# Expert stage of a fused diffusion layer: weight buffers of their own, four slab loads and three splits placed in the selection stage, expert 0's one-hot built tile by tile

## The chip, the cores and the metric

One core of one Trainium2 chip runs the whole program in one launch. The metric is the device time of that launch in microseconds; the kernel before has 3 runs with a median of 3424.07 (3421.85 to 3424.37). Engines are named as in the profile: PE is the matrix engine (PEld its weight loads), DVE the vector engine, ACT the scalar engine, POOL the GpSimd engine, and SP the engine that only issues DMAs here.

## The reference, cut to what matters

The layer runs a pooling and attention mixer over 2048 noisy and 128 context tokens, and then an expert-choice mixture of experts. Only the second part is touched:

```
def ec_moe(h, w_router, w_gate, w_up, w_down):
    xf = h.reshape(N, D)                                  # D = 1024
    aff = softmax(xf @ w_router)                          # 16 experts
    cap = CAPACITY_FACTOR * N // N_EXPERTS                # 256 noisy, 16 context tokens
    gates, idx = lax.top_k(aff.T, cap)
    xe = xf[idx]
    hid = silu(einsum(xe, w_gate)) * einsum(xe, w_up)
    ye = einsum(hid, w_down) * gates[..., None]
    out = zeros((N, D)).at[idx.reshape(-1)].add(ye)
```

## The kernel before, in words

Four stages follow one another, each a block that all engines enter and leave together: the head groups (to about 1815 us of the traced execution), the output projection with the router (to 2076), the selection (`stage_select`, L1992) and the experts (`stage_experts`, L2209).

**Selection.** For every expert the threshold of its 256 best tokens is found bit by bit, three bits a round, in ten rounds. One round on DVE: a comparison of 2048 affinities with a bound, with their count (L2102), the same for the 128 context tokens, a comparison of the two counts with the capacities (`ind`, L2105), a small matmul on PE (L2196), and then `digit` (L2109), `bound` (L2112) and `cand` (L2114), which the next round's comparison waits for (`settled`). `ind`, `bound` and `cand` each read two operands from SBUF and touch 2 elements a partition. After the rounds come masks, ranks by PE, and `g.place`, the slot of every token at every expert. POOL makes the constants, clears the semaphores of the stage before, and is then idle; ACT makes three copies (L2161) and is idle; SP has nothing to do.

**Experts.** Each of the 16 experts has 12 weight slabs of 1024 x 256 values (4 pairs of gate and up, 4 of down), 1 MB each. SP loads slab s into one of RAW = 4 places of `raw` (L2306). For float32 precision each slab is split in two halves: ACT casts it to the high part (L2475), then DVE subtracts that from the slab for the low part (L2567), into one of RING = 3 places of `w`. PE needs both (`w_lo`). SP loads a slab once the slab four before it has been split.

Before expert 0 can start, its tokens have to be found and fetched. DVE makes `hot`, for 16 tiles at once a comparison of the 256 slot numbers with `g.place` (`one_hot(0)`, L2531), then `hot_p`, `vcur` and `hot_all` (L2622, the context tokens of all experts). PE multiplies `hot` and `vcur` to a list of tokens (`make_list`, L2352), DVE turns it into indices (`read_list`, L2547), and POOL gathers the 256 rows by two indirect DMAs (L2321). PE meanwhile picks the context tokens of all experts (`pick`, L2365), split by ACT (L2479) and DVE (`picked`, L2573), transposes the gathered rows (`turn`, L2378), and ACT (L2491) and DVE (L2578) split them into `xT`. Only then come the main matmuls (L2405): 48 a slab.

The order of this beginning is written out by hand for each engine. On DVE: `one_hot(0)`, `hot_all`, `read_list(0)`, four `picked`, two slab splits, four `turned`. On ACT: four `picked`, two slab casts, `place_prompt`, four `turned`. On SP: the loads of `h2p` (0.5 MB) and of `gate2` (twice 0.5 MB), then slabs 0 to 3. The buffers `raw`, `w`, `h2p` and `gate2` are allocated inside the expert stage.

Of the kernel before, what the change touches and what calls it, by code (L numbers as in the profile page):

```python
# [20 lines left out]
F32 = mybir.dt.float32  # L21
F32R = mybir.dt.float32r
BF16 = mybir.dt.bfloat16
U32 = mybir.dt.uint32
ALU = mybir.AluOpType
# [37 lines left out]
def clear_spent(pool, sems):  # L63

    for s in sems:
        pool.sem_clear(s)
# [1922 lines left out]
            run_tiles(pool, body)  # L1989


def stage_select(nc, g, held):  # L1992


    ROUNDS, STEPS = 10, 8
# [1 line left out]
    with ExitStack() as ctx:  # L1997
# [41 lines left out]
        spent, g.spent = g.spent, sems  # L2039
        block = ctx.enter_context(nc.Block())  # L2040

        def over_tiles(x, n):
            return x.rearrange("p (o e) -> p o e", o=1).broadcast_to([P, n, NE])

        @block.gpsimd
        def _(pool):
            nc.gpsimd.iota(lane[:], [[1, P]], base=P, channel_multiplier=-1).then_inc(made_lanes, 1)
            nc.gpsimd.iota(offset[:, 0:1], [[0, 1]], base=0, channel_multiplier=1).then_inc(made_lanes, 1)
            for n, value in enumerate((1.0, float(RATIO))):
                nc.gpsimd.memset(ones[:, n, :], value).then_inc(set_up, 1)  # L2050
            pool.wait_ge(set_up, 2)
            for n in range(2):
                nc.gpsimd.affine_select(out=tri[:, n, :], in_=ones[:, n, :], compare_op=ALU.is_gt, fill=0.0, base=0,
                                        pattern=[[1, P]], channel_multiplier=-1).then_inc(tri_made, 1)
            nc.gpsimd.iota(g.slots[:], [[1, CAP]], base=1, channel_multiplier=0,
                           allow_small_or_imprecise_dtypes=True).then_inc(iotas, 1)
            nc.gpsimd.iota(g.vals[:, :, :, 0], [[0, NT], [0, NE]], base=0, channel_multiplier=1,
                           allow_small_or_imprecise_dtypes=True).then_inc(iotas, 1)
            nc.gpsimd.iota(g.vals[:, :, :, 1], [[1, NT], [0, NE]], base=0, channel_multiplier=0,
                           allow_small_or_imprecise_dtypes=True).then_inc(iotas, 1)  # L2060
            nc.gpsimd.memset(g.tile_off[:], 0.0).then_inc(iotas, 1)
            pool.wait_ge(iotas, 4)
            nc.gpsimd.memset(g.tile_off[:, 0:1], float(T)).then_inc(iotas, 1)
            clear_spent(pool, spent)

        @block.vector
        def _(dve):
# [88 lines left out]
        @block.scalar  # L2156
        def _(act):
            for n in (0, 2, 4):
                act.wait_ge(turned, n + 1)
                src = ps_w[:, n, :] if n < 4 else ps_rp[:, 0:P]  # L2160
                nc.scalar.copy(affT[:, 512 * n:min(512 * n + 512, NT * P)], src).then_inc(turned_s, 1)  # L2161

        @block.tensor
        def _(pe):
# [44 lines left out]
def stage_experts(nc, g, io, outs):  # L2209


    SLABS = 12
    RAW, RING = 4, 3
    TILES = ((0, P), (CAPP, P), (CAPP + P, P))
    sems = []
    with ExitStack() as ctx:  # L2216
        def sb(name, shape, dt=F32):
            return ctx.enter_context(nc.sbuf_tensor(name, shape, dt))
# [2 lines left out]
            sems.append(ctx.enter_context(nc.semaphore(name)))  # L2221
            return sems[-1]

        raw = sb("e_raw", [P, RAW, 2048])
        w = sb("e_w", [P, RING, 2, 2048], F32R)
        hot = sb("hot", [P, NS, CAP], BF16)
        hot_p = sb("hot_p", [P, CAPP], BF16)
        vcur = sb("vcur", [P, NT, 5], BF16)
        found = sb("found", [P, 3, 5])
        gsum = sb("gsum", [P, 3])  # L2230
# [3 lines left out]
        i_cur = sb("i_cur", [P, 3], U32)  # L2234
        xg = sb("xg", [P, 2, D])

        h2p = sb("h2_prompt", [P, D])
        hot_all = sb("hot_all", [P, NE, CAPP])
        xTp = sb("xT_prompt", [P, NE, 2, KD, CAPP], F32R)
        xT = sb("xT", [P, 2, KD, SLOTS], F32R)  # L2240
# [2 lines left out]
        hid = sb("hid", [P, 2, KD, SLOTS], F32R)  # L2243
        yT = sb("e_yT", [P, 2, 2, SLOTS])
        y = sb("e_y", [P, 3, D])
        gate2 = sb("gate2", [P, 2, D])
        ps_gu = ctx.enter_context(nc.psum_tensor("ps_gu", [P, 4, 512], F32))
        ps_d = ctx.enter_context(nc.psum_tensor("ps_d", [P, 3, 512], F32))
        ps_x = ctx.enter_context(nc.psum_tensor("ps_x", [P, 512], F32))

        raw_in = [sem(f"raw_in{q}") for q in range(RAW)]
        w_hi, w_lo, slab_done = sem("e_whi"), sem("e_wlo"), sem("slab_done")
        gate2_in = sem("gate2_in")
        moved, hot_done, listed, found_done, idx_done, gs1, gs2 = (
            sem(n) for n in ("e_moved", "hot_done", "listed", "found_done", "idx_done", "gs1", "gs2"))
        gathered, xT_ready, xT_hi, xT_lo = sem("gathered"), sem("exT_ready"), sem("exT_hi"), sem("exT_lo")
        h2p_in, hot_all_done, xT_placed = sem("h2p_in"), sem("hot_all_done"), sem("exT_placed")
        xTp_ready, xTp_hi, xTp_lo = sem("xTp_ready"), sem("xTp_hi"), sem("xTp_lo")
        silu_done, h32_done, hid_hi, hid_lo = (sem(n) for n in ("silu_done", "eh32_done", "hid_hi", "hid_lo"))
        yT_ready, yT_copied, yT_turned = sem("yT_ready"), sem("yT_copied"), sem("yT_turned")  # L2260
# [28 lines left out]

        @block.sync  # L2290
        def _(sp):
            sp.dma_start(h2p[:], g.h2[NS * P:NT * P, :]).then_inc(h2p_in, 16)
            sp.dma_start(gate2[:, 0, :], g.mod[0, 5 * D:6 * D].partition_broadcast(P)).then_inc(gate2_in, 16)
            sp.dma_start(gate2[:, 1, :], g.mod[1, 5 * D:6 * D].partition_broadcast(P)).then_inc(gate2_in, 16)

            def body(e, before, more):
                for s in range(SLABS):
                    n = SLABS * e + s
                    wait_positive(sp, w_lo, n - RAW + 1)
                    if not isinstance(e, int):  # L2300
                        sp.sem_inc(passed, 1)
                    name, q = ("w_down", s - 8) if s >= 8 else ("w_gate" if s % 2 == 0 else "w_up", s // 2)
                    src = io[name][0].rearrange("e (k p) n -> e p k n", p=P)
                    src = src[bass.ds(e, 1), :, :, 256 * q:256 * q + 256]
                    dst = raw[:, s % RAW, :].rearrange("p (k n) -> p k n", n=256)
                    sp.dma_start(dst, src.rearrange("o p k n -> (o p) k n")).then_inc(raw_in[s % RAW], 16)  # L2306

            run_experts(sp, body)

# [36 lines left out]
        def _(pe):  # L2346
# [45 lines left out]
            def body(e, before, more):  # L2392
# [51 lines left out]
                if not more:  # L2444
                    turn_back(e, 3)

            make_list(0)
            for p in range(PAIRS):
                pick(p)
            for p in range(PAIRS):  # L2450
                turn(0, p)
            pe.wait_ge(xTp_lo, PAIRS)
# [12 lines left out]
        def _(act):  # L2465
            def split(e, s, more):

                if s >= SLABS:
                    if not more:
                        return  # L2470
                    e, s = e + 1, s - SLABS
                wait_positive(act, raw_in[s % RAW], 16 * (3 * e + s // RAW + 1))
                if not (isinstance(e, int) and e == 0 and s < RING):
                    wait_read(act, e, s - RING)
                nc.scalar.copy(w[:, s % RING, 0, :], raw[:, s % RAW, :]).then_inc(w_hi, 1)  # L2475

            def picked(p):
# [37 lines left out]

            for p in range(PAIRS):
                picked(p)
            for s in range(2):
                split(0, s, True)
            place_prompt(0)  # L2520
            for p in range(PAIRS):
                turned(0, p)
# [3 lines left out]
        def _(dve):  # L2526
            def one_hot(e):

                wait_positive(dve, listed, e)
                at = g.place[:, :, bass.ds(e, 1)]  # L2530
                nc.vector.tensor_tensor(hot[:], g.slots[:].rearrange("p (o c) -> p o c", o=1).broadcast_to([P, NS, CAP]),  # L2531
                                        at[:, 0:NS].broadcast_to([P, NS, CAP]), ALU.is_equal).then_inc(hot_done, 1)
                nc.vector.tensor_tensor(hot_p[:], g.slots[:, 0:CAPP],
                                        at[:, NS].broadcast_to([P, CAPP]), ALU.is_equal).then_inc(hot_done, 1)
                nc.vector.tensor_copy(vcur[:], g.vals[:, :, bass.ds(e, 1), :].rearrange("p t o c -> p t (o c)")
                                      ).then_inc(hot_done, 1)

            def read_list(e):

# [19 lines left out]
                nc.vector.tensor_copy(g_cur[:], g_next[:]).then_inc(moved, 1)  # L2559

            def split(e, s, more):
                if s >= SLABS:
                    if not more:
                        return
                    e, s = e + 1, s - SLABS
                wait_positive(dve, w_hi, SLABS * e + s + 1)
                nc.vector.tensor_tensor(w[:, s % RING, 1, :], raw[:, s % RAW, :], w[:, s % RING, 0, :].bitcast(F32),  # L2567
                                        ALU.subtract).then_inc(w_lo, 1)
# [25 lines left out]
            def body(e, before, more):  # L2594
# [22 lines left out]
                    result(e, 1)  # L2617

            nc.vector.memset(found[:], float(NS)).then_inc(found_set, 1)
            dve.wait_ge(found_set, 1)  # L2620
            one_hot(0)
            nc.vector.tensor_tensor(hot_all[:], g.slots[:, 0:CAPP].rearrange("p (o c) -> p o c", o=1).broadcast_to(  # L2622
                [P, NE, CAPP]), g.place[:, NS, :].rearrange("p (e o) -> p e o", o=1).broadcast_to([P, NE, CAPP]),
                ALU.is_equal).then_inc(hot_all_done, 1)
            read_list(0)
            for p in range(PAIRS):
                picked(p)
            for s in range(2):
                split(0, s, True)
            for p in range(PAIRS):  # L2630
                turned(0, p)
            dve.wait_ge(gate2_in, 32)
# [3 lines left out]
def build(nc, io, outs, stop=None):  # L2636
# [7 lines left out]
    with ExitStack() as ctx:  # L2644
# [14 lines left out]
        g.tile_off = sb("tile_off", [P, 3])  # L2659
        stage_output(nc, g, io, outs, after_output)  # L2660
        after_heads.close()
        stage_select(nc, g, after_select)
        after_output.close()
        stage_experts(nc, g, io, outs)
        after_select.close()
# [53 lines left out]
```

## Time and profile before

| | us |
|---|---|
| median of 3 runs | 3424.07 |
| span of the profiled execution | 3423.3 |
| PE busy in it | 3208.2 |
| DVE busy | 2301.4 |
| ACT busy | 1633.2 |
| POOL busy | 633.3 |
| selection stage (start of its first work to the experts' first) | 2076.3 to 2128.7 |
| experts' beginning, to the first main matmul | 2128.7 to 2151.1 |

The span runs from the first to the last instruction of the profiled execution; 0.8 us lie between it and the median of the runs. Times of single instructions below are microseconds from the span's start. "Idle before" with an arrow names what the engine waited for. The granted TensorE clock is given as a share of its full 2.4 GHz, so 0.50 is 1.2 GHz.

### The profile page before, as it was taken

How to read it: one execution, taken by the hardware profiler on the slowest of the kernel's cores; microseconds unless marked ns; L12 is line 12 of the kernel's file. 1: busy time of each engine (PE TensorE's matmuls, PEld its weight loads, DVE VectorE, ACT ScalarE, POOL GpSimd, SP SyncE). 2: the span in 40 equal slices, each digit the busy share in tenths (PEclk: the TensorE clock that was granted, in tenths of full speed). 3: DMA queues.
4: the chain of work that ended last, by engine and by line, in shares of the span. 5: the costliest groups of instructions: out<-in, count | busy, mean ns of one | idle time of the engine just before them, and what ended most of it. 6: DMA issues, size and time to landing. Idle time of an engine off the chain costs nothing. (4 is left out here: it accounts for less than half of the span.)

```text
span 3423.3 us, 69668 instructions
## 1 busy us (share of the span) xinstructions
PE 3208.2 (94%) x23738; PEld 2997.6 (88%) x23738; DVE 2301.4 (67%) x3793; ACT 1633.2 (48%) x3631; POOL 633.3 (18%) x854
## 2 busy tenths in 40 slices
PE   6879999999999999998987993999999999999997
PEld 4879988998998998997775883999999999999997
DVE  4778878877887887887884446555565555555553
ACT  3436656666665665665552110444444444444442
POOL 2432233232223223321000000000110000000001
PEclk8989999999999999999998995999999999999998
DMA  8554444444345435442325551666666666666663
GB/s 281 204 197 141 125 123 151 122 127 152 121 119 157 122 122 165 120 124 93 101 71 220 191 190 57 212 187 185 185 185 195 191 194 194 185 185 185 185 187 86
DMA packets 357398, 542.47 MB, mean 158 GB/s; under 512 B 26266, under 2 KB 280730, under 8 KB 342042
## 3 DMA queue, kind: packets, MB, share of 16 engines
q1 hardware_dynamic: 347548, 506.30, 45.8%
q0 software_dynamic: 9728, 34.61, 4.4%
q8 instruction: 68, 1.11, 0.1%
q14 instruction: 54, 0.44, 0.0%
HBM read 439.10 MB, written 101.74 MB: 158 GB/s over the span
## 5 line engine op out<-in xcount | busy, mean ns | idle before, releaser
L2405 PE MATMUL ps_gu<-xT,e_w 128*128 128x272 f32 x6144 | 789.2, 290 | 2.5 <-DVE xT L2578 2.5
L2405 PEld LDWEIGHTS ps_gu<-xT,e_w 128*128 128x128 f32 x6144 | 779.8, 189 | 3.2 <-issue 2.9
L2567 DVE TENSOR_TENSOR e_w<-e_raw,e_w 128x2048 fp32r<-128x2048 f32 x192 | 440.1, 2292 | 418.1 <-ACT e_w L2475 403.0
L1040 ACT ACTIVATE e<-ps_s,negm 128x1024 f32<-128x1024 f32 (+2 forms) x416 | 473.8, 1145 | 221.4 <-DVE negm L1374 221.4
L1366 DVE TENSOR_REDUCE mx<-ps_s 128x1 f32<-128x1024 f32 (+3 forms) x428 | 521.7, 1232 | 69.0 <-PE ps_s L703 67.5
L703 PE MATMUL ps_s<-kT,qT 128*128 128x512 f32 (+1 forms) x1920 | 469.2, 384 | 12.2 <-ACT e L1040 11.6
L743 PE MATMUL ps_m<-v,aT 128*128 128x128 f32 x3456 | 473.4, 280 | 6.2 <-ACT aT L1028 3.6
L743 PEld LDWEIGHTS ps_m<-v,aT 128*128 128x128 f32 x3456 | 422.6, 192 | 35.2 <-issue 14.6
L703 PEld LDWEIGHTS ps_s<-kT,qT 128*128 128x128 f32 x1920 | 346.9, 190 | 83.9 <-ACT e L1040 17.4
L2424 PE MATMUL ps_gu<-hid,e_w 128*128 128x272 f32 x3072 | 412.1, 291 | 0.0
L773 PE MATMUL ps_m<-w,hT 128*128 128x384 f32 x2040 | 392.8, 340 | 3.9 <-DVE o L1423 3.9
L2424 PEld LDWEIGHTS ps_gu<-hid,e_w 128*128 128x128 f32 x3072 | 392.5, 188 | 0.0
L2475 ACT CAST e_w<-e_raw 128x2048 fp32r<-128x2048 f32 x192 | 365.4, 1903 | 2.7 <-DMA e_raw<-w_up 0.8
L773 PEld LDWEIGHTS ps_m<-w,hT 128*128 128x128 f32 x2040 | 349.9, 188 | 5.4 <-issue 5.4
L1359 DVE SCALAR_TENSOR_TENSOR e<-e,coef 128x512 f32<-128x512 f32 (+1 forms) x480 | 309.7, 693 | 3.4
L1028 ACT COPY aT<-ps_t 128x512 f32<-128x512 f32 (+2 forms) x390 | 203.4, 531 | 210.5 <-PE ps_t L724 210.1
L724 PE MATMUL ps_t<-ident,e 128*128 128x128 f32 x1728 | 270.9, 277 | 13.2 <-DVE e L1359 9.4
L724 PEld LDWEIGHTS ps_t<-ident,e 128*128 128x128 f32 x1728 | 199.5, 141 | 42.4 <-DVE e L1359 24.0
L1885 PE MATMUL ps_y<-wo,cat_o 128*128 128x512 f32 x816 | 199.3, 401 | 19.5 <-DMA cat_o<-cat_d 17.2
L1885 PEld LDWEIGHTS ps_y<-wo,cat_o 128*128 128x128 f32 x816 | 154.0, 192 | 52.4 <-DMA cat_o<-cat_d 18.0
L1253 POOL TENSOR_TENSOR r<-ms,nhalf 128x4 f32<-128x4 f32 x102 | 110.4, 1082 | 473.9 <-ACT ms L1052 473.7
L2504 ACT CAST hid<-e_h 128x544 fp32r<-128x544 f32 x64 | 41.5, 648 | 316.6 <-DVE e_h L2610 316.6
(286 smaller groups left out, 3395.5 us busy)
## 6 DMA issues: line engine op xcount, KB each, us to landing
hT<-hT_d SPq DMA_DIRECT2D x85, 1024.0 KB, 5.6
e_raw<-w_gate SPq DMA_DIRECT2D x64, 1024.0 KB, 5.3
e_raw<-w_up SPq DMA_DIRECT2D x64, 1024.0 KB, 5.2
e_raw<-w_down SPq DMA_DIRECT2D x64, 1024.0 KB, 7.4
qT_d<-qT_out SPq DMA_DIRECT2D x96, 256.0 KB, 5.6
qT<-qT_d SPq DMA_DIRECT2D x96, 256.0 KB, 2.8
tab<-tabs_d SPq DMA_DIRECT2D x85, 256.0 KB, 2.7
hT_d<-hT SPq DMA_DIRECT2D x17, 1024.0 KB, 3.9
```

Of the source, the lines that this page charges most:

```text
L703: mm = nc.tensor.matmul(ps_s[:, at + x - lo:at + y - lo], lhs, keys, start=(half == 0), stop=(half == 1))
L724: mm = nc.tensor.transpose(ps_t[:, n % 2, m * P:m * P + P], src[:, b * P:b * P + P], g.ident[:])
L743: mm = nc.tensor.matmul(ps_m[:, 0:P], aT[:, n % 2, m * P:m * P + P], vals, start=(b == 0), stop=(b == last))
L773: mm = nc.tensor.matmul(projected(s), hT[:, s.par, a, k, :], w[:, s.h % 2, b, k, :], start=(k == 0 and a + b == 0), stop=(k == KD - 1 and ...
L1040: nc.scalar.activation(out, src, ACT.Exp, bias=negm[:, s.par, c:c + 1], scale=HD ** -0.5, accum_out=acc).then_inc(exp_done.sem, 1)
L1359: nc.vector.scalar_tensor_tensor(a, b, coef[:], a, ALU.mult, ALU.add).then_inc(mixed.sem, 1)
L1366: nc.vector.tensor_reduce(mx[:, c, n:n + 1], ps_s[:, at:at + hi - lo], AX, ALU.max).then_inc(mx_part.sem, 1)
L1885: mm = nc.tensor.matmul(ps_y[:, par, half, :], cat[:, par, k, a, :], w[:, b, k, 512 * half:512 * half + 512], start=(k == 0 and a + b == 0 ...
L2405: mm = nc.tensor.matmul(ps_gu[:, 2 * (s % 2) + f, 0:SLOTS], w_view(s, a)[:, k, f * P:f * P + P], xT[:, b, k, :], start=(k == 0 and a + b = ...
L2424: mm = nc.tensor.matmul(ps_gu[:, 2 * (d % 2) + f, 0:SLOTS], w_view(s, a)[:, k, f * P:f * P + P], hid[:, b, k, :], start=(k == 0 and a + b ...
L2475: nc.scalar.copy(w[:, s % RING, 0, :], raw[:, s % RAW, :]).then_inc(w_hi, 1)
L2567: nc.vector.tensor_tensor(w[:, s % RING, 1, :], raw[:, s % RAW, :], w[:, s % RING, 0, :].bitcast(F32), ALU.subtract).then_inc(w_lo, 1)
```

## The change

`open_weights` allocates `e_raw`, `e_w`, `h2_prompt`, `gate2` and their semaphores before the selection stage, in memory that the selection doesn't use. In the selection, SP issues the loads of slabs 0 to 3, of `h2p` and of `gate2`; ACT casts slabs 0 to 2 behind its three copies; POOL, behind its clearing of semaphores, makes the low parts of slabs 0 to 2 (DVE's work before). In the expert stage these are left out, so SP begins with slab 4. DVE makes `hot_all` first, copies expert 0's places to `place_0`, and builds `hot` by 16 instructions of one tile each with a per-partition scalar. PE does `pick(0)` and `pick(1)` before `make_list(0)`; DVE does `picked(0)` before `read_list(0)`.

```diff
+RAW, RING, EARLY = 4, 3, 3
+def open_weights(nc, g, ctx):
+    g.raw = ctx.enter_context(nc.sbuf_tensor("e_raw", [P, RAW, 2048], F32))
+    g.ew = ctx.enter_context(nc.sbuf_tensor("e_w", [P, RING, 2, 2048], F32R))
+    g.h2p = ctx.enter_context(nc.sbuf_tensor("h2_prompt", [P, D], F32))
+    g.gate2 = ctx.enter_context(nc.sbuf_tensor("gate2", [P, 2, D], F32))
...
 def stage_select(...):
+        @block.sync
+        def _(sp):
+            for s in range(RAW):
+                sp.dma_start(g.raw[:, s, :].rearrange("p (k n) -> p k n", n=256), slab_source(io, 0, s)
+                             ).then_inc(g.raw_in[s], 16)
+            sp.dma_start(g.h2p[:], g.h2[NS * P:NT * P, :]).then_inc(g.h2p_in, 16)
+            sp.dma_start(g.gate2[:, 0, :], g.mod[0, 5 * D:6 * D].partition_broadcast(P)).then_inc(g.gate2_in, 16)
+            sp.dma_start(g.gate2[:, 1, :], g.mod[1, 5 * D:6 * D].partition_broadcast(P)).then_inc(g.gate2_in, 16)
...
             clear_spent(pool, spent)
+            for s in range(EARLY):
+                pool.wait_ge(g.w_hi, s + 1)
+                nc.gpsimd.tensor_tensor(g.ew[:, s, 1, :], g.raw[:, s, :], g.ew[:, s, 0, :].bitcast(F32),
+                                        ALU.subtract).then_inc(g.w_lo, 1)
...
+            for s in range(EARLY):
+                act.wait_ge(g.raw_in[s], 16)
+                nc.scalar.copy(g.ew[:, s, 0, :], g.raw[:, s, :]).then_inc(g.w_hi, 1)
...
 def stage_experts(...):
-            sp.dma_start(h2p[:], ...)
-            sp.dma_start(gate2[:, 0, :], ...)
-            sp.dma_start(gate2[:, 1, :], ...)
-                for s in range(SLABS):
+                for s in range(0 if before else RAW, SLABS):
...
+            pick(0)
+            pick(1)
             make_list(0)
-            for p in range(PAIRS):
-                pick(p)
+            pick(2)
+            pick(3)
...
             def split(e, s, more):                      # on ACT and on DVE
+                if isinstance(e, int) and e == 0 and s < EARLY:
+                    return
...
-            for s in range(2):                          # on ACT and on DVE
-                split(0, s, True)
...
+            def first_hot():
+                for t in range(NS):
+                    ins = nc.vector.tensor_scalar(hot[:, t, :], g.slots[:], place_0[:, t:t + 1], None, ALU.is_equal)
+                ins.then_inc(hot_done, 1)
+                nc.vector.tensor_tensor(hot_p[:], g.slots[:, 0:CAPP], g.place[:, NS, 0:1].broadcast_to([P, CAPP]),
+                                        ALU.is_equal).then_inc(hot_done, 1)
+                nc.vector.tensor_copy(vcur[:], g.vals[:, :, 0, :]).then_inc(hot_done, 1)
...
-            dve.wait_ge(found_set, 1)
-            one_hot(0)
             nc.vector.tensor_tensor(hot_all[:], ...).then_inc(hot_all_done, 1)
+            nc.vector.tensor_copy(place_0[:], g.place[:, 0:NS, 0]).then_inc(found_set, 1)
+            dve.wait_ge(found_set, 2)
+            first_hot()
+            picked(0)
             read_list(0)
-            for p in range(PAIRS):
+            for p in range(1, PAIRS):
                 picked(p)
```

## Rows read from the trace of the kernel before

**Rows 1.** The page's first part: busy time of each engine.
```profile
PE 3208.2 (94%) x23738; PEld 2997.6 (88%) x23738; DVE 2301.4 (67%) x3793; ACT 1633.2 (48%) x3631; POOL 633.3 (18%) x854
```

**Rows 2.** The chain of waits from the experts' start, in order of time.
```profile
2130.49 13.66 DMA e_raw<-w_up
...
2144.17 1.91 ACT e_w L2475
...
2146.10 2.29 DVE e_w L2567
...
2151.05 33.12 PE ps_gu L2405 x240
```

**Rows 3.** Busy time by stretch: start:end, length, PE, PEld, DVE, ACT, POOL, clock, DMA, GB/s.
```profile
2090.00:2100.00 10.00, 0.56 (x3) 0.31 (x3) 9.00 (x25) 0.00 (x0) 0.00 (x0) 0.50 0.00 0
...
2151.00:2156.90 5.90, 5.86 (x26) 5.89 (x27) 2.29 (x1) 1.22 (x1) 0.00 (x0) 0.50 1.09 350
2156.90:2160.00 3.10, 3.10 (x26) 3.10 (x26) 0.00 (x0) 0.01 (x1) 0.00 (x0) 0.99 0.48 154
```

**Rows 4.** Timeline of DVE, first of the ten selection rounds: start, length, what.
```profile
2081.72 2.35 DVE L2102 TENSOR_SCALAR_CACHE_REDUCE passing<-affT,bound 128x2048 bf16<-128x2048 f32 x1
...
2084.50 0.16 DVE L2105 TENSOR_TENSOR ind<-count_s,caps 128x2 bf16<-128x2 f32 x1
...
2085.20 0.22 DVE L2112 SCALAR_TENSOR_TENSOR bound<-digit,offset,cand 128x2 uint32<-128x2 uint32 x1
2085.34 0.15 DVE L2114 TENSOR_TENSOR cand<-digit,cand 128x2 uint32<-128x2 uint32 x1
```

**Rows 5.** The page's sixth part: loads of a slab, median us to landing.
```profile
e_raw<-w_gate SPq DMA_DIRECT2D x64, 1024.0 KB, 5.3
```

**Rows 6.** Timeline of ACT: its idle time before its first work for the experts.
```profile
2136.69 0.59 ACT L2479 CAST xT_prompt<-ps_d 128x512 fp32r<-128x512 f32 x1 [55.36 <-issue]
```

**Rows 7.** Groups of instructions on POOL, shapes apart: busy, mean ns of one.
```profile
L1270 POOL TENSOR_TENSOR sinp<-qkn,tab 128x128 f32<-128x128 f32 x204 | 90.4, 465 | 0.0
...
L1264 POOL TENSOR_TENSOR cosp<-qkn,tab 128x256 f32<-128x256 f32 x102 | 75.0, 735 | 466.6 <-DVE qkn L1387 466.6
```

**Rows 8.** Line 1535 alone: instructions with the least, median and longest ns.
```profile
L1535 DVE TENSOR_TENSOR e<-e,edge x16: 157/164/669, 105.9 to 244.5; 64x8 f32<-64x8 f32 x16
```

**Rows 9.** Timelines of DVE and of POOL, 226.0 to 228.2.
```profile
226.45 0.91 DVE L1537 SCALAR_TENSOR_TENSOR e<-e,inv_w 64x512 f32<-64x512 f32 x1
227.39 0.59 DVE L1535 TENSOR_TENSOR e<-e,edge 64x8 f32<-64x8 f32 x1
...
225.47 1.34 POOL L1270 TENSOR_TENSOR sinp<-qkn,tab 128x128 f32<-128x128 f32 x2
226.94 1.01 POOL L1278 TENSOR_TENSOR rot<-cosp,sinp 128x256 f32<-128x256 f32 x1
```

**Rows 10.** Timeline of SP: the first load of the expert stage.
```profile
2128.67 0.34 SPq L2292 DMA_DIRECT2D h_prompt<-h_d  x1
```

**Rows 11.** Timeline of DVE: a copy in the selection, then the experts' one-hots.
```profile
2076.39 0.69 DVE L2083 COPY wide<-aff 128x1024 f32<-128x1024 f32 x1
...
2128.85 4.42 DVE L2531 TENSOR_TENSOR hot<-slots,place 128x4096 bf16<-128x4096 bf16 x1
...
2133.39 0.41 DVE L2622 TENSOR_TENSOR hot_all<-slots,place 128x256 f32<-128x256 bf16 x1
```

**Rows 12.** Timeline of POOL: the second of the two gathers for expert 0.
```profile
2136.93 0.96 POOL L2321 DMA_INDIRECT xg<-h_d,i_next  x1 [0.30 <-issue]
```

**Rows 13.** The gathered tile `xg`, all 16 experts: issue to landing.
```profile
DMA to landing us min/median/max: 4.9/5.3/7.9
```

**Rows 14.** Timelines of PE and of ACT: transposes of expert 0's rows, last copy.
```profile
2144.82 3.68 PE L2378 MATMUL ps_gu<-ident,xg 128*128 128x128 f32 x16 [3.92 <-DMA xg<-h_d,i_next]
...
2148.54 0.59 ACT L2491 CAST xT<-ps_gu 128x512 fp32r<-128x512 f32 x1 [0.27 <-PE ps_gu L2378]
```

**Rows 15.** Timeline of DVE: the splits of expert 0's rows.
```profile
2148.31 2.48 DVE L2578 TENSOR_TENSOR xT<-ps_gu,xT 128x512 fp32r<-128x512 f32 x4
```

More of the change, by code:

```diff
@@ L1989, in _, with slab_source, stage_select @@
             run_tiles(pool, body)
-def stage_select(nc, g, held):
+RAW, RING, EARLY = 4, 3, 3
[4 more added lines that the diff above has]
+    g.gate2 = ctx.enter_context(nc.sbuf_tensor("gate2", [P, 2, D], F32))
+    g.raw_in = [ctx.enter_context(nc.semaphore(f"raw_in{q}")) for q in range(RAW)]
+    g.w_hi, g.w_lo, g.h2p_in, g.gate2_in = (
+        ctx.enter_context(nc.semaphore(n)) for n in ("e_whi", "e_wlo", "h2p_in", "gate2_in"))
+def slab_source(io, e, s):
+    name, q = ("w_down", s - 8) if s >= 8 else ("w_gate" if s % 2 == 0 else "w_up", s // 2)
+    src = io[name][0].rearrange("e (k p) n -> e p k n", p=P)
+    return src[bass.ds(e, 1), :, :, 256 * q:256 * q + 256].rearrange("o p k n -> (o p) k n")
+def stage_select(nc, g, io, held):
     ROUNDS, STEPS = 10, 8
@@ L2212, in stage_experts @@
     SLABS = 12
-    RAW, RING = 4, 3
     TILES = ((0, P), (CAPP, P), (CAPP + P, P))
@@ L2222, in sem @@
             return sems[-1]
-        raw = sb("e_raw", [P, RAW, 2048])
-        w = sb("e_w", [P, RING, 2, 2048], F32R)
+        raw, w, h2p, gate2 = g.raw, g.ew, g.h2p, g.gate2
         hot = sb("hot", [P, NS, CAP], BF16)
         hot_p = sb("hot_p", [P, CAPP], BF16)
+        place_0 = sb("place_0", [P, NS])
         vcur = sb("vcur", [P, NT, 5], BF16)
@@ L2235, in stage_experts @@
         xg = sb("xg", [P, 2, D])
-        h2p = sb("h2_prompt", [P, D])
         hot_all = sb("hot_all", [P, NE, CAPP])
@@ L2245, in stage_experts @@
         y = sb("e_y", [P, 3, D])
-        gate2 = sb("gate2", [P, 2, D])
         ps_gu = ctx.enter_context(nc.psum_tensor("ps_gu", [P, 4, 512], F32))
@@ L2249, in stage_experts @@
         ps_x = ctx.enter_context(nc.psum_tensor("ps_x", [P, 512], F32))
-        raw_in = [sem(f"raw_in{q}") for q in range(RAW)]
-        w_hi, w_lo, slab_done = sem("e_whi"), sem("e_wlo"), sem("slab_done")
-        gate2_in = sem("gate2_in")
+        raw_in, w_hi, w_lo, h2p_in, gate2_in = g.raw_in, g.w_hi, g.w_lo, g.h2p_in, g.gate2_in
+        sems.extend(raw_in + [w_hi, w_lo, h2p_in, gate2_in])
+        slab_done = sem("slab_done")
         moved, hot_done, listed, found_done, idx_done, gs1, gs2 = (
@@ L2256, in stage_experts @@
         gathered, xT_ready, xT_hi, xT_lo = sem("gathered"), sem("exT_ready"), sem("exT_hi"), sem("exT_lo")
-        h2p_in, hot_all_done, xT_placed = sem("h2p_in"), sem("hot_all_done"), sem("exT_placed")
+        hot_all_done, xT_placed = sem("hot_all_done"), sem("exT_placed")
         xTp_ready, xTp_hi, xTp_lo = sem("xTp_ready"), sem("xTp_hi"), sem("xTp_lo")
@@ L2291, in _ @@
         def _(sp):
-            sp.dma_start(h2p[:], g.h2[NS * P:NT * P, :]).then_inc(h2p_in, 16)
-            sp.dma_start(gate2[:, 0, :], g.mod[0, 5 * D:6 * D].partition_broadcast(P)).then_inc(gate2_in, 16)
-            sp.dma_start(gate2[:, 1, :], g.mod[1, 5 * D:6 * D].partition_broadcast(P)).then_inc(gate2_in, 16)
             def body(e, before, more):
-                for s in range(SLABS):
+                for s in range(0 if before else RAW, SLABS):
                     n = SLABS * e + s
@@ L2301, in body @@
                         sp.sem_inc(passed, 1)
[L2302 to L2306, printed above, removed]
+                    sp.dma_start(raw[:, s % RAW, :].rearrange("p (k n) -> p k n", n=256), slab_source(io, e, s)
+                                 ).then_inc(raw_in[s % RAW], 16)
             run_experts(sp, body)
@@ L2472, in split @@
                 wait_positive(act, raw_in[s % RAW], 16 * (3 * e + s // RAW + 1))
-                if not (isinstance(e, int) and e == 0 and s < RING):
-                    wait_read(act, e, s - RING)
+                wait_read(act, e, s - RING)
                 nc.scalar.copy(w[:, s % RING, 0, :], raw[:, s % RAW, :]).then_inc(w_hi, 1)
@@ L2561, in split @@
             def split(e, s, more):
+                if isinstance(e, int) and e == 0 and s < EARLY:
+                    return
                 if s >= SLABS:
@@ L2624, in _ @@
                 ALU.is_equal).then_inc(hot_all_done, 1)
+            nc.vector.tensor_copy(place_0[:], g.place[:, 0:NS, 0]).then_inc(found_set, 1)
+            dve.wait_ge(found_set, 2)
+            first_hot()
+            picked(0)
             read_list(0)
-            for p in range(PAIRS):
+            for p in range(1, PAIRS):
                 picked(p)
-            for s in range(2):
-                split(0, s, True)
             for p in range(PAIRS):
@@ L2661, in build @@
         after_heads.close()
-        stage_select(nc, g, after_select)
+        open_weights(nc, g, ctx)
+        stage_select(nc, g, io, after_select)
         after_output.close()
```

## The prediction

> **What bounds the kernel now.** The page comes first: PE is busy for 94% of the span, so most of the program is not at stake [rows 1]. The change touches two stretches in which PE has little to do, and each has its own limit. In the selection the view by stretch shows DVE busy 9.00 of 10 us and PE 0.56: ten rounds in which one small DVE instruction waits for the one before [rows 3]. Whatever delays one of them delays the program. In the experts' beginning the chain of waits names the weights: the second slab landed 13.66 us after its issue, ACT cast it (1.91), DVE split it (2.29), DVE's four splits of the tokens followed, and the main matmuls began at 2151.05 [rows 2]. From there PE runs without a gap (240 matmuls in 33.12 us, the first ones slow by their clock), so only what comes before 2151.05 can be gained.
>
> **What the early weights save.** Loads, casts and splits of slabs 0 and 1 leave the chain. Next in line is the gather. Its rows were there at 2144.82, when PE began 3.68 us of transposes, and ACT's last copy ended at 2149.13 [rows 14]. One of DVE's four splits costs 2.48 / 4 = 0.62 [rows 15]; with 0.25 for the start of PE this gives 2150.0, that is 5.2 after the landing. Today's 2151.05 is thus 1.05 later than the gather alone would give, and this much is sure. The rest hangs on when the gather lands.
>
> Its issue hangs on the list, and that on `hot`, 4.42 us for 4096 elements, one element a cycle [rows 11]. In its place stand `hot_all` first (0.41 busy, some 0.34 until the next can start), a copy of 16 elements (0.2) and 16 instructions of 256 elements. No row has this form. By the rate of `hot`, 4.42 / 16 = 0.28 and some 0.06 of start make 0.34 each, 5.4 in all, and the list 1.6 later; by the copy of 1024 elements in 0.69, two elements a cycle, it is 0.14 and 0.06, 3.2 in all, and the list 0.6 earlier. The new form has one tensor input, as that copy has, so I take 3.2 (down to 2.2 if it ran at twice that rate, which nothing in the rows excludes). The Trainium skill (VectorE: DVE Perf Modes, Mode 4×_2P) says that a tensor_scalar whose tensors are all 16-bit and in SBUF goes at four elements a cycle; by it the list is some 1.6 earlier. The trace has no such instruction.
>
> The second gather goes out at 2136.93 and landed 7.9 later, the longest of 32; the median is 5.3 [rows 12, 13]. What made it long was 5.5 MB queued in front and around it from 2128.67 on [rows 10]. Now `h2p`, `gate2` and four slabs are already there, but SP does not wait: the splits of slabs 0 to 2 are done, so slabs 4 to 6, 3 MB, go out at 2128.67. At the 350 GB/s of [rows 3] they keep the DMA engines busy to about 2139, and the gather, issued at 2136.3, still meets them. So its wait lies between 4.9 and 7.9; I take 6.0, and the landing at 2142.3 (2141.2 to 2144.2). With the 5.2 from above the main matmuls start 2147.5 after an unchanged selection: **3.5 us earlier**, between 1.5 and 5.5.
>
> At no cost: two `pick`s before the list (four matmuls of 256 columns, some 1.8 us by the 3.68 for twice as many columns in [rows 14]; PE waits for `hot` at that time, also if it took 2.2 only); `picked(0)` before `read_list` (0.69, under the list's matmuls); ACT's three casts, 5.7 us inside an idle time of 55.4 [rows 6]; SP's seven issues in a stage where it does nothing. Slab 3 and all later ones are split under PE's work as before, and with three more slabs loaded ahead nothing there gets later.
>
> The clock: from 2151.0 to 2156.9 the granted clock was 0.50, then 0.99, and 26 matmuls took 5.90 and 3.10 us [rows 3]; the low stretch therefore costs 2.9. PE's pattern before it (picks, a gap, transposes, a gap) stays much the same, so I leave it at no change; at best 2.9 come back, at worst another 0.5 goes.
>
> **What the early splits cost.** DVE's subtraction is now POOL's, during the rounds. POOL needs 465 ns for 128 columns and 735 for 256 [rows 7], hence 2.11 ns a column, and for 2048 columns 465 + 1920 x 2.11 = 4.5 us; three take 13.5. POOL is idle then, and they end far ahead of the stage. What counts is what DVE does meanwhile. Line 1535 shows it: an instruction with two inputs in SBUF on 8 columns, 164 ns as a rule and once 669 [rows 8]. [Rows 9] show one such place. The one at 227.39 took 0.59 and ended at 227.98, just behind POOL's 256 columns of 226.94, which ended at 227.95. Those took 1.01 in place of 0.735, as they had themselves met DVE's instruction of 226.45 to 227.36, and that had begun beside POOL's pair, which ended at 226.81. I read this as turns: whoever comes second waits for the whole instruction, however small its own.
>
> In a selection round `ind`, `bound` and `cand` have two SBUF inputs [rows 4]. The first slab lands 5.3 after its issue at 2076.3 [rows 5], ACT casts it in 1.9, so POOL's first subtraction starts near 2083.5; the other casts (one each 3 us, the time of 1 MB at 350 GB/s) are ready before POOL wants them. Then:
> - POOL 2083.5 to 2088.0: `ind`, due at 2084.50, waits 3.5.
> - POOL's second to 2092.6: `bound`, due 0.7 after `ind`, waits 3.9.
> - POOL's third to 2097.1: `cand`, queued behind `bound`, waits 4.5.
>
> Together **11.9 us**, all on the chain, since PE and the next comparison wait for them. The bounds: nothing, if tiny DVE instructions slip in between POOL's accesses; 14, if the long comparison (one SBUF input and a count) is held as well. If `bound` and `cand` pass together between two subtractions, or POOL starts some 2 us later, the comparison of 2.35 runs beside POOL and about 3 are saved: 8 to 9. On that upper bound the Trainium skill (SBUF — State Buffer, Who interferes with whom) says that a tensor_scalar which also writes its accumulator doesn't compete with GpSimd; by it the 14 is ruled out. No row shows such an instruction beside POOL's work, so the bound stays.
>
> **Sum.** 3423.3 + 11.9 - 3.5 = 3431.7 for the profiled execution; the median of the runs shown lies 0.8 above that execution's span, so **3432.5**. A measurement of this kernel can tell some 0.2%, 6.8 us, from no change, so 3430.9 is where "slower" begins.
>
> **The rivals.**
> 1. POOL and DVE don't hold each other here (not slower). The places in [rows 9] are few and short; if a long subtraction of POOL lets instructions of 2 elements through, the cost of the selection vanishes and the prologue's gain stays: 3424.1 - 3.5 = 3420.6. It decides from the point at which the rounds lose less than 3.5 us. Against it: the 8-column instruction that waited. 12%.
> 2. They hold each other less than in the sum: the comparison covers part of each subtraction, 8 us, and the gather lands near the median: 3424.1 + 8 - 4.5 = 3427.6. 25%.
> 3. The change doesn't shorten the gather: slabs 4 to 6 stand in front of it just as slabs 0 to 3 did, 7.9 again, landing at 2144.2, and only some 1.6 are gained: 3424.1 + 11.9 - 1.6 = 3434.4. For it: the queue was full at that moment too. 18%.
> 4. The clock rises before the main matmuls and the selection isn't held: 3420.6 - 2.9 = 3417.7, just over 0.2% faster only with the best gather as well. 5%.
>
> The forecast, 3432.5, has 40%.
>
> **How the numbers follow.** The forecast's own range is 3429 to 3436. The held cases reach from 3425 to 3437.5; to hold the time 8 times in 10 I go down to 3420.5, rival 1's time, as its sign is the other. Slower by over 0.2% are rival 3, most of the forecast and a little of rival 2: 0.58. Faster by over 0.2% is the best part of rival 4: 0.05. The rest, 0.37, is within.
>
> **What would show it.** In the profile after: POOL's three subtractions of 128x2048 at some 4.5 us each between 2083 and 2098; `ind`, `bound` or `cand` of the first round or two with 3 to 4.5 us in place of 0.2; the experts' first load near 2140.6 for 2128.7 [rows 10]; between this and the first main matmul 18.9 us for 22.4, with PE's transposes waiting for the gather, not for weights; `hot` as 16 instructions at 0.2 us from start to start. Wrong would be: rounds that keep their pace beside POOL's work (then rival 1), or a main stage that now waits for slab 3 or later.

## The result, and the profile after

The changed kernel takes 3428.09 us (median of 20 runs, 3424.22 to 3432.61) where the kernel before took 3423.81 (20 runs, 3420.26 to 3426.88): ratio 1.0014, 95% interval 1.0008 to 1.0020. It is slower, by 4.3 us, which lies within the 0.2% that were called "no change". The forecast was 3432.5. The profiled execution has a span of 3428.6, against 3423.3.

First the page's part on busy time, for [rows 1], then DVE's timeline of the first selection rounds, for [rows 4]:

```profile
PE 3205.6 (93%) x23738; PEld 2994.9 (87%) x23738; DVE 2301.1 (67%) x3806; ACT 1633.7 (48%) x3631; POOL 643.8 (19%) x857
```
```profile
2085.50 3.82 DVE L2139 TENSOR_TENSOR ind<-count_s,caps 128x2 bf16<-128x2 f32 x1
...
2089.86 3.92 DVE L2146 SCALAR_TENSOR_TENSOR bound<-digit,offset,cand 128x2 uint32<-128x2 uint32 x1
2093.70 0.15 DVE L2148 TENSOR_TENSOR cand<-digit,cand 128x2 uint32<-128x2 uint32 x1
...
2096.67 1.58 DVE L2139 TENSOR_TENSOR ind<-count_s,caps 128x2 bf16<-128x2 f32 x1
```

The busy totals hide it. POOL has 10.5 us more, for its three subtractions; DVE has as much as before, as three of its own subtractions went away (2.29 us each, [rows 2]) and the time that it was held counts as busy. Three small instructions show all: 0.16, 0.22 and 0.16 us before, 3.82, 3.92 and 1.58 now, together 8.8 more. POOL's timeline has its subtractions beside them, and the second gather, for [rows 12]:

```profile
2084.80 13.43 POOL L2097 TENSOR_TENSOR e_w<-e_raw,e_w 128x2048 fp32r<-128x2048 f32 x3 [3.71 <-ACT e_w L2198]
...
2146.03 0.96 POOL L2348 DMA_INDIRECT xg<-h_d,i_next  x1 [0.30 <-issue]
```

The subtractions took 4.5 us each, ending at 2089.3, 2093.8 and 2098.2, and so did `ind`, `bound` and the next `ind`. The experts' beginning, by the chain of waits (for [rows 2]) and by DVE's and SP's timelines (for [rows 11, 10]):

```profile
2146.03 6.29 DMA xg<-h_d,i_next
...
2152.37 3.69 PE ps_gu L2405 x16
2156.08 0.59 ACT xT L2521
2156.70 0.70 DVE xT L2617
...
2157.64 32.30 PE ps_gu L2432 x240
```
```profile
2138.50 0.42 DVE L2659 TENSOR_TENSOR hot_all<-slots,place 128x256 f32<-128x256 bf16 x1 [0.58 <-PEq L2018]
...
2139.04 3.22 DVE L2569 TENSOR_SCALAR hot<-slots,place 128x256 bf16<-128x256 bf16 x16
```
```profile
2138.43 0.38 SPq L2332 DMA_DIRECT2D e_raw<-w_gate  x1
2138.86 0.57 SPq L2332 DMA_DIRECT2D e_raw<-w_up  x1
2139.49 1.38 SPq L2332 DMA_DIRECT2D e_raw<-w_gate  x1
```

No slab is on the chain any more; the gather is. From the start of each stage to the next (DVE's first instruction of a stage, PE's first main matmul), in us:

| | selection | beginning | first main matmul to expert 1's list |
|---|---|---|---|
| before | 52.4 | 22.3 | 33.0 |
| after | 61.15 | 19.15 | 32.1 |
| difference | +8.75 | -3.15 | -0.8 |

These make 4.8 of the span's 5.3; the selection also started 1.0 later, and 0.5 came back behind expert 0, in parts that the change doesn't touch. The second and third of these times move from execution to execution: two more profiles of the kernel before (numbers 9 and 10) have beginnings of 21.5 and 22.1, so the beginning gained 2.3 to 3.2, not exactly 3.15. The selection doesn't move (52.4 each time).

### The profile page after: what moved, and what is told of

Its sections match the earlier page's. It is cut to its first block and busy times, and to the rows that moved or that the text cites. A ratio compares the mean times of both kernels' runs of the same rounds, so it can differ in the third digit from the quotient of the medians.

```text
span 3428.6 us, 69684 instructions
## 1 busy us (share of the span) xinstructions
PE 3205.6 (93%) x23738; PEld 2994.9 (87%) x23738; DVE 2301.1 (67%) x3806; ACT 1633.7 (48%) x3631; POOL 643.8 (19%) x857
## 5 line engine op out<-in xcount | busy, mean ns | idle before, releaser
L2606 DVE TENSOR_TENSOR e_w<-e_raw,e_w 128x2048 fp32r<-128x2048 f32 x189 | 433.0, 2291 | 417.8 <-ACT e_w L2505 417.8
```

## The experiments

Every kernel here is compared with the runs of the kernel before on its own chip. The three durations are measured as in the table above, each in one profile; "after the stage's start" means after DVE's first instruction of the expert stage. Lines that a diff leaves out are marked by `...`.

**1. The low parts made by DVE again.** POOL's loop is left out, the early loads and casts stay, and DVE's `split` no longer skips slabs 0 to 2.

```diff
-            for s in range(EARLY):                  # POOL, in the selection
-                pool.wait_ge(g.w_hi, s + 1)
-                nc.gpsimd.tensor_tensor(...)
...
-            for p in range(1, PAIRS):               # DVE, in the expert stage
-                picked(p)
+            picked(1)
+            split(0, 0, True)
+            picked(2)
+            picked(3)
+            split(0, 1, True)
```

> The changed kernel without POOL's three subtractions: the slabs are still loaded and cast early, but DVE makes the low parts, of slabs 0 and 1 between its splits of the context tokens (where it is idle for 1.3 and 5.3 us now, waiting for ACT and for the gather) and of slab 2 in the loop. Theory (POOL's subtractions hold DVE's small instructions, and that is the whole loss): all ten rounds back at 3.74 us, selection 52.3 us instead of 61.1, and 8.8 us off the changed kernel's time; from the experts' start to the main matmuls 18 to 19.5 us, as SP now waits for DVE's first split before it loads slab 4, and the gather meets fewer loads. Median some 3418.5 to 3420, faster than both. Rival (the early DMA traffic or ACT's casts slow the rounds): the rounds stay at their loss of 8.8 or a part of it, and the time stays at 3426 or above.

Measured: selection 52.39, no instruction held, so the early traffic and ACT's casts cost nothing, and POOL's subtractions are the whole loss. But the time was 3421.39 (11 runs; before 3422.67; ratio 0.9994, 0.9985 to 1.0003), which can't be told from the kernel before, and the beginning took 20.37, 0.9 above the range that was expected. The timelines of POOL, DVE and SP say why:

```profile
2136.99 2.09 POOL L2344 DMA_INDIRECT xg<-h_d,i_next  x1 [0.30 <-issue]
...
2135.97 2.28 DVE L2600 TENSOR_TENSOR e_w<-e_raw,e_w 128x2048 fp32r<-128x2048 f32 x1
...
2138.28 0.38 SPq L2328 DMA_DIRECT2D e_raw<-w_gate  x1
```

Now DVE holds POOL: the making of the second gather took 2.09 in place of 0.96 beside a DVE subtraction that ended at 2138.25, and PE's transposes began 15.1 after the stage's start, not 13.9. Of this 1.2, the longer making is 1.1. The queue was empty when the gather went out, but didn't stay so: with its first split done SP issued slab 4 at 2138.28, before the making of the gather ended (2139.08). From that end to the transposes it took 5.6 us, for 5.4 in the changed kernel and 4.3 in number 5, where no slab moved meanwhile.

The hold doesn't rest on this one place. At the end of each expert POOL makes indirect DMAs that scatter `y_sample`. In the trace of the kernel before, one such instruction took 3.04 us the first time and 2.29 to 2.31 the 13 later times, always beside a split of DVE that had begun first (timelines of POOL and DVE, two of the places):

```profile
2248.26 3.04 POOL L2332 DMA_INDIRECT y_sample<-e_y,i_cur  x1 [0.31 <-issue]
...
2247.57 2.29 DVE L2567 TENSOR_TENSOR e_w<-e_raw,e_w 128x2048 fp32r<-128x2048 f32 x1 [1.08 <-ACT e_w L2475]
...
2327.11 2.29 POOL L2332 DMA_INDIRECT y_sample<-e_y,i_cur  x1 [0.30 <-issue]
...
2325.67 2.29 DVE L2567 TENSOR_TENSOR e_w<-e_raw,e_w 128x2048 fp32r<-128x2048 f32 x1 [1.08 <-issue]
```

Both end 1.4 us behind the end of DVE's split (2249.87 and 2327.96). Where DVE's subtraction began second, POOL wasn't stretched: the making of the first gather in number 1 took its usual 1.20, though the subtraction began 0.5 into it.

**2. POOL as busy, but only writing.** The low parts of slabs 0 to 2 are zero here.

```diff
-                nc.gpsimd.tensor_tensor(g.ew[:, s, 1, :], g.raw[:, s, :], ..., ALU.subtract)
+                nc.gpsimd.memset(idle[:, s, :], 0.0)
+                nc.gpsimd.memset(g.ew[:, s, 1, :].bitcast(F32), 0.0)
```

> The changed kernel with POOL's subtractions replaced by POOL instructions that only write: per slab one memset of 3072 columns into an unused buffer and one of 2048 into the low part, some 4.5 us a slab as before. The low parts of slabs 0 to 2 are zero, so expert 0's products leave that part out. Theory (DVE instructions with two SBUF inputs compete with POOL's reads alone): the rounds run at 3.74 us beside 13.5 us of POOL work, selection 52.3 us. Rival (any POOL work in SBUF holds them): ind and bound wait 3.5 to 4 us again, selection near 61.

Measured: selection 52.39. POOL was busy beside the rounds (first line, of its timeline), and `ind` and `bound` (of DVE's) took what they always had:

```profile
2079.80 2.66 POOL L2098 MEMSET idle<- 128x3072 f32 x1 [3.63 <-ACT e_w L2199]
...
2080.57 0.16 DVE L2140 TENSOR_TENSOR ind<-count_s,caps 128x2 bf16<-128x2 f32 x1
...
2081.28 0.22 DVE L2147 SCALAR_TENSOR_TENSOR bound<-digit,offset,cand 128x2 uint32<-128x2 uint32 x1
```

So it isn't POOL's work as such. A memset differs from the subtraction in that it reads nothing, and that is the likely reason; a POOL instruction that reads a single input wasn't run. The single time, 3415.0, also holds an early start of the selection (4 us) and a fast expert 0.

**3. Each subtraction in 8 pieces of 256 columns.**

> The changed kernel with each POOL subtraction cut into 8 of 256 columns. Theory (they take turns by whole instructions): ind, bound and cand each wait for one piece at most, 0.7 us and 0.4 on average, in the four or five rounds that POOL's work of 17 us now spans; the selection loses 3 to 7 us, no single wait over 0.9 us. Rival (what counts is POOL's busy time, however it is cut): 8.8 us or more lost.

Measured: selection 55.9, 3.5 us lost in seven waits, the time 3423.8 (one run). DVE's timeline:

```profile
2084.11 0.62 DVE L2141 TENSOR_TENSOR ind<-count_s,caps 128x2 bf16<-128x2 f32 x1
...
2085.26 0.22 DVE L2148 SCALAR_TENSOR_TENSOR bound<-digit,offset,cand 128x2 uint32<-128x2 uint32 x1
2085.40 0.70 DVE L2150 TENSOR_TENSOR cand<-digit,cand 128x2 uint32<-128x2 uint32 x1
...
2090.13 0.74 DVE L2150 TENSOR_TENSOR cand<-digit,cand 128x2 uint32<-128x2 uint32 x1
```

POOL was busy for longer (16.4 us for 13.4) and cost less. No wait exceeds a piece (0.73): they take turns by instructions, and the length of POOL's sets the price.

**4. Halves, started behind `cand` of one of the first six rounds.**

```diff
-            for s in range(EARLY):
...
+            for j in range(2 * EARLY):
+                s, at = j // 2, 1024 * (j % 2)
+                pool.wait_ge(g.w_hi, s + 1)
+                pool.wait_ge(step, 8 + 6 * (j + 1))       # cand of round j
+                ins = nc.gpsimd.tensor_tensor(g.ew[:, s, 1, at:at + 1024], ..., ALU.subtract)
```

> The changed kernel with each POOL subtraction cut in two halves of 1024 columns (2.36 us by 465 + 896 x 2.11 ns), each of them started behind cand of one of the first six rounds, that is beside the comparison of 2048 values with its count (2.35 us and 0.5 more until ind). Theory (only ind, bound and cand are held; the comparison isn't): no wait at all, selection 52.3 us, the experts' beginning as in the changed kernel at 19.2 us: 8.8 us off, median near 3419.3. Rival (the comparison is held as well, as it also reads SBUF): each half adds some 2.4 us, selection near 66 us, median near 3433.

Measured: selection 52.39, beginning 19.14, 3418.81 us (11 runs; before 3422.67; ratio 0.9985, 0.9976 to 0.9994). The timelines of POOL and DVE:

```profile
2085.65 2.35 POOL L2099 TENSOR_TENSOR e_w<-e_raw,e_w 128x1024 fp32r<-128x1024 f32 x1 [5.55 <-DVE cand L2152]
2089.38 2.35 POOL L2099 TENSOR_TENSOR e_w<-e_raw,e_w 128x1024 fp32r<-128x1024 f32 x1 [1.38 <-DVE cand L2152]
...
2085.53 2.35 DVE L2140 TENSOR_SCALAR_CACHE_REDUCE passing<-affT,bound 128x2048 bf16<-128x2048 f32 x1
```

The long comparison ran beside them in the 2.35 us that it takes alone. It isn't held, and the same work on POOL at another moment is free.

**5. Slab 4 held back until the gathered rows are there.**

```diff
+                    if not before and s == RAW:
+                        sp.wait_ge(xT_ready, 1)
```

> The changed kernel with SP holding slab 4 (and so 5 and 6) back until PE has transposed the first pair of expert 0's gathered rows. Theory (the three slabs issued at the stage's start stand in front of the gather; PE's first transpose came 13.9 us after the stage's start, the second gather's issue 7.5): with the DMA engines empty the gather needs 4.0 to 4.9 us from the second issue instead of 6.3, PE's transposes start 11.5 to 12.4 us after the stage's start, and the beginning falls from 19.2 to some 17.2 us. Rival (the gather's own 1 MB and its making on POOL set the time): 13.9 and 19.2 as before. A cost could appear later: a PE wait for slab 4 in expert 0; slab 4 then lands some 18 us after the stage's start and is needed some 40 us after it, so none is expected. The selection keeps its loss of 8.8 us.

Measured: transposes 12.8 after the stage's start, beginning 17.9, selection 61.0, and 3426.4 us in a single run. Of the 2 us expected, 1.2 came: the chain has 5.21 from the second issue to the landing for 6.29. With slabs queued the gather's first bytes come 4.1 us behind the first issue and the rest within 3.1; alone the first come at 1.9, but the rest takes 4.3 (the second half is only issued 1.5 after the first).

**6. Halves and held slab together.**

> Both at once: POOL's subtractions in halves beside the comparisons (selection 52.4 us measured with it) and SP holding slab 4 back. Theory: selection 52.4 and beginning 17.2, so 2 us under the kernel with the timed halves alone (3418.8), near 3416.8, and 6 to 7 us under the kernel before. Rival: holding back gives nothing, 3418.8.

Measured: selection 52.4, beginning 17.9, 3417.72 us (11 runs; before 3424.30; ratio 0.9981, 0.9972 to 0.9990): 6.6 us under the kernel before, the best version here. Over number 4 it gains 1.2 in the beginning; by ratios of the two (0.9981 to 0.9985) that isn't clear of noise.

**7. The one-hot in one instruction again.**

> The changed kernel with expert 0's one-hot as one DVE instruction again, everything else as changed. The 16 instructions took 3.22 us, the one 4.42. Theory: the list and the gather's issue come 1.1 to 1.2 us later (second issue 8.7 instead of 7.5 us after the stage's start), but the gather's first bytes wait for the three slabs anyway (they came 4.1 us after the first issue), so PE's transposes start only 0 to 0.6 later and the beginning takes 19.2 to 19.8. Rival: the delay goes through whole, 20.3.

Measured, DVE's timeline and the chain of waits:

```profile
2139.58 4.43 DVE L2568 TENSOR_TENSOR hot<-slots,place 128x4096 bf16<-128x4096 bf16 x1
```
```profile
2147.60 5.26 DMA xg<-h_d,i_next
```

The second issue came 8.56 after the stage's start in place of 7.53, the transposes at 13.9 and the beginning 19.15, both as in the changed kernel (single run: 3428.9 us). The gather waited a microsecond less in the queue. The tile-by-tile one-hot is faster and gains nothing in this kernel.

**8. The changed kernel once more.**

> The changed kernel once more, unchanged. In its profile cand started 13 ns before POOL's third subtraction and slipped through with bound. If that is a matter of a few ns, it may be held this time (its 0.15 us become some 4.4, and the selection loses 11.9 instead of 8.8); if the order of the two is fixed by how they wait, ind 3.8, bound 3.9, cand 0.15 and the next ind 1.6 come again within 0.3 us.

Measured: selection 60.9, beginning 19.1, 3425.1 us (one run); DVE's timeline:

```profile
2082.23 3.55 DVE L2139 TENSOR_TENSOR ind<-count_s,caps 128x2 bf16<-128x2 f32 x1
2086.32 3.92 DVE L2146 SCALAR_TENSOR_TENSOR bound<-digit,offset,cand 128x2 uint32<-128x2 uint32 x1
2090.16 0.15 DVE L2148 TENSOR_TENSOR cand<-digit,cand 128x2 uint32<-128x2 uint32 x1
2093.12 1.58 DVE L2139 TENSOR_TENSOR ind<-count_s,caps 128x2 bf16<-128x2 f32 x1
```

`cand` began 19 ns ahead of POOL's third subtraction, and 21 and 9 ns in numbers 5 and 7. This order repeats with whole subtractions. It isn't safe, though: in number 3 `cand` twice began 4 and 3 ns ahead of POOL's next piece and was held all the same (0.74 us at 2090.13, the last line shown there).

**9 and 10. The kernel before, twice more, for the clock.**

> The kernel before once more, for the clock in expert 0. From the first main matmul to expert 1's list PE needs 32.96 us in its profile; in the changed kernels it was 32.14 once, 31.95 to 31.74 three times and 30.34 five times. Theory A (where the clock rises is chance, and differs from execution to execution of one kernel): this one differs from 32.96 by over 0.3 us. Theory B (the change moved it): 32.7 to 33.3 again, and the change brought 0.8 to 2.6 us by the clock alone. The selection and the beginning: 52.4 and 22.3 again.

> The same kernel a third time, for the same question: by theory A some value between 30.3 and 33.3 us that needn't agree with the other two, by theory B 32.7 to 33.3.

Measured: 33.1 and 31.85 us, beginnings of 21.5 and 22.1, selections of 52.4, times of 3423.3 and 3423.7 us. Number 9 alone fits theory B; number 10 doesn't. So executions of one kernel differ by 1.2 here, and theory B in its narrow form fails. The changed kernel shows the same, by stretches of 5.4 us from the first main matmul, in the profile above and in number 8:

```profile
2157.60:2163.00 5.40, 5.36 (x28) 5.39 (x29) 0.00 (x0) 0.36 (x1) 0.00 (x0) 0.62 0.01 3
```
```profile
2154.00:2159.40 5.40, 5.34 (x42) 5.37 (x43) 0.00 (x0) 0.38 (x1) 0.00 (x0) 1.00 0.01 3
```

28 matmuls at a granted clock of 0.62, 42 at 1.00, with the same instructions ahead. Yet the shortest value, 30.3, came in five of the nine profiles of changed kernels and in none of three of the kernel before. The time that PE is idle just before the main matmuls doesn't explain it by itself: it is 1.6 to 1.7 us in all nine, and 2.5, 1.6 and 2.9 in the three, where the profile with 1.6 (number 9) has the slowest expert 0. Whether the change makes the short value likelier stays open; three profiles are too few.

## Why the prediction was right or wrong

- **POOL and DVE hold each other by whole instructions**, read from [rows 8, 9]: right, as numbers 1 to 4 show. The first two waits were put at 3.5 and 3.9 and came out at 3.7 and 3.7.
- **"`cand`, queued behind `bound`, waits 4.5"**: this step failed. `cand` starts 9 to 21 ns ahead of POOL's next subtraction, in all four profiles with whole subtractions, and goes through with `bound`. The third subtraction then runs beside the comparison and holds only the end of it, `ind` by 1.4. The cost was 8.75, not 11.9. The text had this case as a variant at 8 to 9, and chose the other by the turns of [rows 9], where DVE's next instruction was not yet waiting.
- **Is the comparison held?** The bound of 14 left that open, and number 4 closes it: it is not. The Trainium skill (SBUF — State Buffer, Who interferes with whom) says so of a tensor_scalar that writes its accumulator, and the trace agrees (2.35 us beside POOL's work).
- **The beginning**: 18.9 forecast, 19.15 measured; gather 6.3 from its second issue for 6.0. Right also in what bounds it: the slabs in front of the gather (number 5), worth 1.1 of the 6.3.
- **The one-hot**: 3.2 forecast, 3.22 measured. At the four elements a cycle that the Trainium skill (VectorE: DVE Perf Modes, Mode 4×_2P) states for such an instruction it would be an estimated 2.2; here, with 16-bit tensors and a float32 scalar per partition, the trace doesn't agree: 0.20 from start to start for 256 elements, as the two elements a cycle of the copy in [rows 11] gave. Not foreseen was that the 0.6 earlier list would be swallowed by the queue (number 7).
- **Two `pick`s at no cost**: right by little, and the reading was wrong. They were put at four matmuls and 1.8 us, so that they'd be free even with a `hot` of 2.2. In the trace they are eight matmuls and take 3.75 us, from 2139.07 to 2142.82, and the list's first matmul began at 2142.61, when `vcur` had ended at 2142.47. With a `hot` of 2.2 they would have held the list up.
- **The clock at no change**: 0.8 less in the profile, within what executions of one kernel differ by. (The slow stretch of [rows 3] costs 5.90 - 3.10 = 2.8, not 2.9; nothing hangs on it.) In the median the loss is 4.3, and 8.75 - 3.15 gives 5.6. The means of three profiles of the kernel before and two of the changed one differ by +8.6 in the selection, -2.8 in the beginning and -1.4 in expert 0, together 4.4. That fits, but how much of it is the clock isn't shown, as the last term moves by over 1 us between executions of one kernel.
- **Sum**: 3432.5 - 3.15 (`cand`) + 0.35 (the beginning) - 0.8 (clock) gives 3428.9, against 3428.09 measured. The sign was right, the 0.2% were not reached. The time lies 0.9 under the forecast's own range (3429 to 3436) and 0.5 from rival 2's 3427.6, which had the selection nearly right (8) and the gather too early (4.5 gained). So the wider range held the time, and not the forecast's sum.

## What to carry to other kernels

Work moved to an idle engine isn't free if the two hold each other when both read SBUF, as VectorE and GpSimd do here: ask what short instructions of the critical engine have two SBUF inputs, and give GpSimd its reads only beside instructions that don't, in pieces no longer than those. When a load is taken off the chain, look at the queue that is next: three slabs prefetched as early as possible stood in front of a gather and swallowed the microsecond won ahead of it.

## What the runs showed of the hardware

- A DVE instruction on 2 elements a partition waited 3.9 us for a POOL instruction; the same POOL time spent in memsets, which only write, cost nothing, and a comparison with one SBUF input and a count ran beside POOL's subtraction in its usual 2.35 us.
- It works the other way too: POOL's making of an indirect DMA took 2.09 us for 0.96 beside a DVE subtraction that had begun first, and the making of a scatter took 3.04 or 2.29 depending on when DVE's subtraction ended.
- An indirect gather of 1 MB in two halves landed 6.3 us behind its second issue with 3 MB of loads queued ahead, 5.2 on empty DMA engines. Its first bytes came 4.1 and 1.9 us behind its first issue.
